# Six stationary operands moved to other byte addresses in SBUF, in a two-stage projection kernel that TensorE bounds

## The reference, cut to what matters

```python
h = rms_norm(x, norm_mix)
proj = h @ w_in                      # 2048 x 5656, split into three head groups
# gated linear attention, mLSTM and spatial gating on the parts of proj -> mix (256 x 2048)
x = x + mix @ w_out                  # 2048 x 2048
hf = rms_norm(x, norm_ffn)
gate, up = jnp.split(hf @ w_gu, 2, axis=-1)      # 2048 x 11264
x = x + (jax.nn.silu(gate) * up) @ w_down        # 5632 x 2048
return rms_norm(x, norm_final)
```

## Time and profile before

| | |
|---|---|
| median of 2 runs | 1138.97 us (1138.73 to 1139.22) |
| span of the profiled execution, first to last instruction | 1136.7 us |
| PE busy | 1123.7 us, 99% of the span |
| PEld busy | 931.9 us, 82% |
| DVE busy | 628.6 us, 55% |
| ACT busy | 512.6 us, 45% |
| POOL busy | 41.6 us, 4% |
| memory traffic | mean 186 GB/s |
| mean granted clock of TensorE | 0.997 of full speed |

### The profile page before, as it was taken

The page is one execution under the profiler, slowest core; times in us unless marked ns, Lnnn a source line. Parts: engine busy times, 40 slices in busy tenths (PEclk is TensorE's granted clock), DMA queues, the critical chain, the costliest instruction groups (busy, mean ns, idle before and its releaser), DMA issues.

```text
span 1136.7 us, 13836 instructions
## 1 busy us (share of the span) xinstructions
PE 1123.7 (99%) x5211; PEld 931.9 (82%) x5211; DVE 628.6 (55%) x709; ACT 512.6 (45%) x608; POOL 41.6 (4%) x66
## 2 busy tenths in 40 slices
PE   8999999999999999999999999999999999999996
PEld 7898889888888888888888888888888888888885
DVE  5456767698565555555554555555545545454443
ACT  6444535555445544443444443444444334343432
POOL 2700000000010000000000000000000000000000
PEclk9999999999999999999999999999999999999999
DMA  8665646555475576666666666666666555556552
GB/s 277 208 205 150 196 121 195 159 166 151 146 254 180 177 226 200 186 185 192 189 189 188 186 186 199 185 189 189 189 190 187 183 186 187 189 187 188 188 188 93
DMA packets 110058, 211.09 MB, mean 186 GB/s; under 512 B 6844, under 2 KB 11008, under 8 KB 109632
## 3 DMA queue, kind: packets, MB, share of 16 engines
q1 hardware_dynamic: 108960, 205.75, 59.4%
q0 software_dynamic: 1056, 4.77, 1.2%
HBM read 208.40 MB, written 2.10 MB: 185 GB/s over the span
## 4 chain that ended last, share of the span: by engine, by line
PE 98%; DMA 1%; ACT 0%; SPq 0%; DVE 0%; ACTq 0%; issue 0%; POOLq 0%; POOL 0%
PE acc L984 31%; PE acc L986 31%; PE acc L985 31%; PE mx L976 2%; PE mx L1155 1%; PE mx L1061 1%; DMA tok<-in_x 1%; ACT x L544 0%; PE mx L1139 0%; PE mx L1046 0%; PE mx L1183 0%; PE mx L1210 0%; PE acc L1002 0%; SPq L207 0%; PE acc L1003 0%; PE acc L1006 0%
## 5 line engine op out<-in xcount | busy, mean ns | idle before, releaser
L563 DVE TENSOR_TENSOR w_lo<-raw,w_hi 128x1024 fp32r<-128x1024 f32 (+2 forms) x392 | 470.5, 1204 | 472.8 <-ACT w_hi L332 472.3
L332 ACT ACTIVATE w_hi<-raw 128x1024 fp32r<-128x1024 f32 (+2 forms) x392 | 408.1, 1044 | 549.2 <-PE acc L986 539.6
L984 PE MATMUL acc<-w_hi,hT_hi 128*128 128x512 f32 (+2 forms) x1084 | 418.5, 386 | 0.0
L986 PE MATMUL acc<-w_hi,hT_lo 128*128 128x512 f32 (+2 forms) x1084 | 415.5, 383 | 0.0
L985 PE MATMUL acc<-w_lo,hT_hi 128*128 128x512 f32 (+2 forms) x1084 | 415.3, 383 | 0.0
L986 PEld LDWEIGHTS acc<-w_hi,hT_lo 128*128 128x128 f32 x1084 | 203.5, 188 | 40.2
L984 PEld LDWEIGHTS acc<-w_hi,hT_hi 128*128 128x128 f32 x1084 | 203.6, 188 | 39.5 <-ACT tok L357 0.4
L985 PEld LDWEIGHTS acc<-w_lo,hT_hi 128*128 128x128 f32 x1084 | 203.6, 188 | 38.8
L984 PE MATMUL acc<-w_hi,actT_hi 128*128 128x512 f32 x352 | 139.6, 397 | 0.0
L986 PE MATMUL acc<-w_hi,actT_lo 128*128 128x512 f32 x352 | 139.5, 396 | 0.0
L985 PE MATMUL acc<-w_lo,actT_hi 128*128 128x512 f32 x352 | 139.5, 396 | 0.0
(11 more groups left out here) (192 smaller groups left out, 471.3 us busy)
## 6 DMA issues: line engine op xcount, KB each, us to landing
raw<-in_w_gu SPq DMA_DIRECT2D x176, 512.0 KB, 3.7
raw<-in_w_down SPq DMA_DIRECT2D x88, 512.0 KB, 3.9
raw<-in_w_in SPq DMA_DIRECT2D x80, 512.0 KB, 4.3
raw<-in_w_out SPq DMA_DIRECT2D x32, 512.0 KB, 4.2
raw<-in_w_in SPq DMA_DIRECT2D x8, 272.0 KB, 2.9
raw<-in_w_in SPq DMA_DIRECT2D x8, 264.0 KB, 2.8
tok<-in_x SPq DMA_DIRECT2D x8, 256.0 KB, 7.5
x<-in_x POOLq DMA_DIRECT2D x2, 1024.0 KB, 8.8
```

The lines of the kernel that those rows point to most:

```text
L332: act.activation(w_hi[:, slot, 0:UC * width], raw[:, slot, 0:UC * width], ACT.Copy)\
L563: dve.tensor_tensor(w_lo[:, slot, 0:UC * width], raw[:, slot, 0:UC * width], w_hi[:, slot, 0:UC * width].bitcast(F32), ALU.subtract).then_ ...
L984: pe.matmul(o, hi[:, c + i, tb], wh, start=first and i == 0, stop=False)
L986: ins = pe.matmul(o, lo[:, c + i, tb], wh, start=False, stop=last and i == UC - 1)
```

## The change

The change alters only where tensors stand. Two small unused tensors are put ahead of `hT_hi` and `hT_lo`. In `early`, `mixT_hi` and `mixT_lo` are declared ahead of `tok` with an alignment of 512 bytes and a gap between them. In `late`, gaps stand ahead of `actT_hi` and `actT_lo`. The gaps are never read or written.

```diff
-        def sb(name, shape, dt=F32, where=None):
-            return (where or ctx).enter_context(nc.sbuf_tensor(name, shape, dt))
+        def sb(name, shape, dt=F32, where=None, align=32):
+            return (where or ctx).enter_context(nc.sbuf_tensor(name, shape, dt, align_bytes=align))
...
         w_lo = sb("w_lo", [P, R, UC * GW], F32R)
+        sb("gap0", [P, 16])
         hT_hi = sb("hT_hi", [P, KC, T], F32R)
+        sb("gap1", [P, 16])
         hT_lo = sb("hT_lo", [P, KC, T], F32R)
...
         early = ExitStack()
+        mixT_hi = sb("mixT_hi", [P, KC, T], F32R, early, align=512)
+        sb("gap2", [P, 64], where=early)
+        mixT_lo = sb("mixT_lo", [P, KC, T], F32R, early)
         tok = sb("tok", [P, NB, TOKW], where=early)
-        mixT_hi = sb("mixT_hi", [P, KC, T], F32R, early)
-        mixT_lo = sb("mixT_lo", [P, KC, T], F32R, early)
...
         late = ExitStack()
+        sb("gap3", [P, 24], where=late, align=1024)
         actT_hi = sb("actT_hi", [P, FC, T], F32R, late)
+        sb("gap4", [P, 56], where=late)
         actT_lo = sb("actT_lo", [P, FC, T], F32R, late)
```

## The result

The changed kernel takes 1148.72 us (2 runs, 1148.72 to 1148.73) against 1138.97 us: ratio 1.0085, 95% interval 1.0069 to 1.0101. It is slower by 9.8 us, where 5 us less had been forecast. The span of the profiled execution went from 1136.7 to 1147.0 us.

A forecast was written before the change was run, and what follows sets the result against it. PE's matmul spacing was taken as the bound; hT 0, mixT -2.6 and actT -2.7 us sum to 5.3 less than the 1136.7 span, giving 1131.4 and a time of 1134 us. Its own range was 1128 to 1137, the whole range 1127 to 1159.

The forecast's parts named there:

- What bounds the kernel: Whole kernel: PE is always fed, so only the distance from one matmul to the next can change the time noticeably.
- one settled and one unsettled cadence: Matmul streams: settled steps of 226.6 ns, which hT's addresses allow, or unsettled ones of 231 to 236 ns.
- only between starts: mixT and actT matmuls: the extra 7 to 8 ns do not show in the weight load, recorded with 188 ns.
- A stationary tile is cheap when it starts at a multiple of 64 bytes: All stationary tiles: the likeliest rule, others being dear; range by it alone 1128.3 to 1136.4 us.
- altogether wrong: All stages: the case that cadence depends on the distance between stationary and moving tile; no size given.
- hT, forecast 0: hT's 3072 matmuls: hT_hi goes to 64 modulo 128, hT_lo stays at 0, both cheap, so 0 us.
- Rival A: hT stages: 64 is not enough, period 128 bytes or the like; net 9.8 to 18.7 us more, chance 0.30.
- mixT, forecast -2.6: Output projection, 384 matmuls: both tiles go from 32 to 0 modulo 128, 2.6 us less, bounds 0 and 6.6.
- actT, forecast -2.7 by proportion: Down, 1056 matmuls: only actT_lo becomes cheap, a third of the steps gain; 2.7 us less, bounds 0 and 8.1.
- Other engines' buffers, priced at nothing: ACT and DVE buffers at new addresses cost 0; x's wait changes 0 to 1 us either way, taken as 0.
- Rival C: All stages: addresses have nothing to do with the cadences; time stays at 1139 us, chance 0.11.
- The rule of 16-byte lines: SBUF: penalties come with crossing 16-byte lines, so all addresses, multiples of 32, are equally good and the change does nothing.

The follow-up runs named there:

- e9: Kernel before, old placement, with the last three column groups of down not loading, splitting or waiting for weights; 1138.75 us.
- e10: Same cut in down's last three column groups, on the version with all six stationary tensors and both weights at 128 modulo 1024; 1129.03 us.
- e2: Kernel before with mixT ahead of tok, weights moved to 192 modulo 1024, hT kept at 128, mixT at 192, actT at 256; 1141.58 us.
- e1: Kernel before with mixT ahead of tok, high and low alike modulo 1024: hT at 192, mixT at 128, actT at 0, weights at 128; 1154.72 us.
- e4: Kernel before with mixT ahead of tok and gaps putting all six stationary tensors at 128 modulo 1024 like the weights; 1128.55 against 1139.12 us, ratio 0.9905.
- e3: Kernel before with mixT ahead of tok, high tensors at 128 modulo 1024, hT_lo at 256, mixT_lo at 192, actT_lo at 640; 1144.03 us.
- e5: Changed kernel without the two gaps ahead of hT_hi and hT_lo; 1135.9 us against 1139.29 for the kernel before, ratio 0.9972.
- e11: Kernel before with mixT ahead of tok, w_lo at 192 modulo 1024, w_hi at 128, hT at 192, mixT at 128, actT_hi 192, actT_lo 128; 1159.64 us.

## Why the prediction was wrong

**What bounds the kernel.** Right. PE alone sets the time, no other engine's time changed, and the time went where the distance between starts went. e9 and e10 showed that the cadence is PE's own. The picture of one settled and one unsettled cadence, "of 231 to 236 ns", was too simple: there are many cadences, 228.9 at distance 192 and 228.3 at 240 among them, and the stream keeps each as steadily as 226.7. The sentence that the extra time shows "only between starts" is right for the weight loads and wrong for the matmuls, whose recorded durations grow too (last section).

**"A stationary tile is cheap when it starts at a multiple of 64 bytes."** This is the step that failed. It was chosen as the smallest rule that divides three cadences, and it looked at the stationary address alone. In e2 that address modulo 1024 stays and the cadence changes; in e1 multiples of 64 and of 1024 run at 233.3 and 232.4. What decides is the distance to the weights, modulo 256. All three cadences of before fit that as well: 0, 32 and 96. The clue was in the table of addresses: hT and the weights had the same residue modulo 1024. The prediction even named the distance as a way to be altogether wrong, and then passed over it because the classes modulo 128 are the same by either reading. That is true, the weights being at a multiple of 128, but the coarser class decides: mixT, which goes to a multiple of 128, is 128 away from the weights modulo 256. And modulo 128 too, hT_hi went to a class, 64, that the rule called cheap and that e1 shows dear (hT at 192: 233.3).

**hT, forecast 0.** Measured +12.9 us over the two stages with hT. Rival A, with a chance of 0.30, had this outcome in outline (hT_hi becomes dear) and named the right stage, and its net, 9.8 to 18.7 us, has the measured 9.8 at its lower edge. That edge was reached by other terms, though: A had two thirds of the steps lose 6.7 ns and mixT gain 2.6 us, where all steps lose 4.4 ns on average and mixT and actT together gain 2.5. Its cause, a period of 128 of the tile's own address, was not the right one either. The result lies inside the range of the whole (1127 to 1159) only because that range took in A; the direction and the size of the forecast were those of the wrong case.

**mixT, forecast -2.6.** Measured -0.3: 232.4 ns instead of 233.3, since -128 and +128 are unsettled too. e4 gives what was forecast, at distance 0: the output projection there takes 100.3 us instead of 102.7.

**actT, forecast -2.7 by proportion.** Measured -2.2. The size came out near by chance: actT_hi was taken to stay as dear as before and actT_lo to become cheap, but both moved to other distances, -32 and +192, one dear and one among the cheapest of the unsettled places, for a mixed cycle of 232.2 ns. Mixed cycles are not in proportion in general. The table's cadences, weighted two to one, would give 233.0 ns for hT of the changed kernel and 228.6 for hT of e3; both measured 231.1.

**Other engines' buffers, priced at nothing.** Right: e5 leaves no room for a cost there. x's wait became 0.5 us shorter, inside the 1 us allowed, but the clock's later rise took more than that back.

**Rival C's argument** that the plain float32 matmuls run at 216 ns although kT is as badly placed as mixT is no longer one: kT stands right behind qT, which is 4096 bytes long, and each product reads the same columns of both, so their distance is 0 modulo 256.

**The rule of 16-byte lines** (the Trainium skill, page "SBUF — State Buffer", section "Door 1: The DMA port swizzle"), as the prediction applied it, said that the change has no effect. For addresses that are all multiples of 32 the runs differ from the kernel before by up to 21 us (e11). The measurement decides: for this pair of streams 16 bytes are not the unit. The Trainium skill (page "SBUF — State Buffer", section "Who interferes with whom") also says that PE has two independent read ports, one for the moving operand and one for the weight load, and never waits on anyone. e9 and e10 agree in that PE's cadence is the same with and without the other engines' work (234.3 and 226.7 ns); but a dependence on the distance between the two operands is hard to square with their independence.

**What stays open.** That the two streams meet in the same part of the memory is argued from the dependence on both addresses and from e9, not shown: no run separates the weight load from the matmul beside it. Nor is it shown why a settled step takes 226.7 ns, nor what chooses between two cadences at the same distance (16, 128, 208).

## What to carry to other kernels

When PE is the bound and back-to-back matmuls of one shape run at different cadences in different stages, compare the byte addresses of both operands, not of one: here a difference of 0 modulo 256 between stationary and moving tiles gave 226.7 ns in every case, and the eleven other differences 228 to 235 (16 at times 226.7). The cure costs two gaps of 672 bytes (e4) and gained 1% of this kernel's time. Where three cadences can be divided by several rules, one that uses a difference deserves the same weight as one that uses a single address, and an experiment that moves the *other* operand tells them apart in one run.

## What had not been expected of the hardware

A stream of equal matmuls has a memory: behind an interruption its steps are irregular, for up to about ten of them, and then it falls into a cycle that it keeps for hundreds. At distance 0 this is one step of 226.7 ns; at 96 it has seven steps of 231 to 238 ns, at -64 three of 225 to 232. At +16, two cycles are possible at the same addresses (226.7 and 233.3 ns), and the choice can change from one restart to the next. The two most frequent means, 226.7 and 233.3, are 6.7 ns apart, 16 periods at 2.4 GHz. The weight load itself is recorded with 187 to 190 ns on average in every one of these cycles, so its duration does not show the loss. The matmul's does, though it overlaps the next one. Down's high tile, before (distance 96) and in e4 (distance 0), busy us and mean ns:

```profile
L984 PE MATMUL acc<-w_hi,actT_hi 128*128 128x512 f32 x352 | 139.6, 397 | 0.0
```

```profile
L986 PE MATMUL acc<-w_hi,actT_hi 128*128 128x512 f32 x352 | 137.0, 389 | 0.0
```

The 7 to 8 ns are there, but in a duration of 390 they are 2% and easily passed over; the starts give them directly.
